# The w_out product's first row tile done in pieces between the last band heads

## The chip, the cores and the metric

The kernel runs on one core of a Trainium2 chip. The metric is the device time of one execution in microseconds (us). Five engines work side by side, each through its own queue in order, and wait for each other by semaphores: TensorE (PE), VectorE (DVE), ScalarE (ACT), GpSimd (POOL) and SyncE (SP, which here issues DMAs).

## The reference, cut to what matters

One layer of a hybrid encoder works on 1024 prompt rows and on 8 running streams (samples) of 16 rows each, 1152 rows in all, 1024 wide:

```
h   = rms_norm(x, g0)
... = split(h @ w_in)
o_fox  = fox_attention(q, k, v, log forget)   # 4 heads, causal, with the samples' cache of 256
o_lru  = rglru_block(...)
o_band = band_attention(q, k, v, rel_bias)    # 4 heads; a chunk of 64 sees itself and 8 before it
mix = concat([o_fox, o_lru, o_band]) @ w_out  # 1024 x 1024
x   = x + rms_norm(mix, g1)
h2  = rms_norm(x, g2)
gate, val = split(h2 @ w_up)
x   = x + rms_norm((gelu(dwconv(gate)) * val) @ w_down, g3)
```

All is float32. A big product is done in three passes of reduced type: each operand is split into a high part (a copy, by ACT) and a low part (value minus high part, by DVE), and PE sums high x high, high x low and low x high.

## The kernel before

The rows are cut into nine tiles of 128: 0 to 7 are the prompt, 8 the samples. After the w_in products comes the attention, a list of 44 units (`attention_steps`, `STEPS`, two steps each), written out by hand in `FOX_ORDER`, `BAND_ORDER` and two lists of places. A unit of kind pf or pb is two heads of one row tile q of the prompt (fox or band); pf needs q+1 blocks of 128 keys, pb at most five (q=0 one, q=1 two, q=2 three, q=3 four). Units sf and sb are two times two sample streams; kf, kb and kt turn keys.

The band's part was, as units 24 to 43: q=4, 4, 3, 3, key turn, 5, key turn, 5, sb (unit 32), 2, 2, 6, 6, sb (unit 37), 1, 1, 7, 7, 0, 0. Unit numbers m are those of the loop `for m in range(NUNIT)`, which each engine has.

All engines run through the units with a software pipeline. In iteration m

- PE turns the probabilities of unit m's first step (`turn_probs`), makes the scores of unit m+2 (`scores`), turns those of m's second step, and multiplies the turned ones of the unit before m with the values (`values`).
- DVE normalises the first step of m+1, takes both score tiles of m+2 out of PSUM with bias and row minimum (`take_scores`, L1226), normalises the second step of m+1 (L1237, L1246) and copies the output of the unit before m to `mix` (`take_output`, L1260).
- ACT copies the turned probabilities of m from PSUM (`turned_back`, L865) and exponentiates those of m+1 and m+2 (L873), or copies turned keys (L880).

`scores(m+2)` needs PSUM banks that DVE (or ACT, for keys) has taken unit m+1 from.

w_out is loaded by SP in eight halves q of 128 x 1024 elements (512 KB) into two buffers `raw`; load q waits for the low split of q-2. A split of a half is ACT's `split_hi` (L751) and DVE's `split_lo` (L1018). Halves 0 to 5 were split behind units 37 to 42 (`OUT_SPLITS`, from the last sb unit on, because w_hi and w_lo take the place of the samples' keys), 6 and 7 behind the loop. There also `mix_hi` (L909) and `mix_lo` (L1018) split the row tiles of `mix` into `act_hi` and `act_lo`; three tiles are split ahead. These buffers take the place of the keys, the values and the bias, so the first of them waited for the last output.

Then PE multiplies tile by tile, in the order 0 to 8, 48 matmuls each (L1731), and turns the finished row tile before it (`turn_y2`, L1426). For a tile ACT squares and takes the root (L945, L947), DVE multiplies with gains (L1326), adds the old rows `x_res` (L1329), ACT squares again (L952), DVE makes y2 (L1335); PE's turned y2 is split again (L930, L1018) and is the operand of the w_up product (L1436), which starts with the first six tiles. SP issues, behind the last w_out half: gains twice (when the last values are done), two halves of w_up (when w_out's halves 6 and 7 are split), x_res of tile 0, and then one x_res per tile.

```
            values(NOUT - 1)
...
            pe.wait_ge(att_out_used, NOUT)
            pe.wait_ge(w_lo_ready, R_OUT + 4)
            for t in range(NT):
                pe.wait_ge(lo_ready, NT + t + 1)
```

Of the kernel before, what the change touches and what calls it, by code (L numbers as in the profile page):

```python
# [119 lines left out]
def attention_steps():  # L120
# [21 lines left out]
    among_band = list(zip(pairs_of("kt") + pairs_of("sb"), (4, 5, 6, 10)))  # L142
# [5 lines left out]
BAND_ORDER = (4, 3, 5, 2, 6, 1, 7, 0)  # L148
# [14 lines left out]
OUT_SPLITS = [LAST["sb"] // 2 + q for q in range(6)]  # L163
# [66 lines left out]
def encoder_step(nc, i, o):  # L230
    with ExitStack() as ctx:
# [85 lines left out]
        with ExitStack() as s:  # L317
            wx_hi = sb("wx_hi", [P, 2048], F32R, s)
            wx_lo = sb("wx_lo", [P, 2048], F32R, s)
            x_res = sb("x_res", [P, D], F32, s)  # L320
            x1 = sb("x1", [P, D], F32, s)
            y2 = sb("y2", [P, D], F32, s)
# [150 lines left out]
        def mixed_banks(t):  # L473

            return 6 if t % 2 == 0 else 2

        def ring(r, tiles, spare):


            assert COUNT[FIRST["pb"]] % 4 == 0  # L480
# [30 lines left out]
        def _(sp):  # L511
# [26 lines left out]
            for q in range(8):  # L538
                r = R_OUT + q
                h, k0 = q // 4, 2 * (q % 4)  # L540
                if q == 0:
# [3 lines left out]
                          w_out[k0 * P:(k0 + 2) * P, h * 512:(h + 1) * 512].rearrange("(k p) c -> p k c", p=P))  # L545
# [43 lines left out]
        def _(pool):  # L589
# [131 lines left out]
            for t in range(NT):  # L721
                pool.wait_ge(x1_ready, t + 1)
                pool.dma_start(x1_dram[t * P:(t + 1) * P, :], x1[:, :]).then_inc(x1_stored, 16)
# [16 lines left out]
        def _(act):  # L740
# [150 lines left out]
            for m in range(NUNIT):  # L891
# [36 lines left out]
            def h2_half(t):  # L928
                act.wait_ge(y2_turned, t + 1)
                act.activation(act_hi[:, :, t * P:(t + 1) * P],  # L930
# [83 lines left out]
        def _(dve):  # L1014
# [247 lines left out]

            take_scores(0)
            take_scores(2)
            for m in range(NUNIT):
# [25 lines left out]
            def mix_lo(t):
                cols = slice(t * P, (t + 1) * P)
                dve.wait_ge(hi_ready, NT + t + 1)
                subtract(act_lo[:, :, cols], mix[:, :, cols], act_hi[:, :, cols]).then_inc(lo_ready, 1)
# [15 lines left out]
            def h2_lo_half(t):  # L1310
                cols = slice(t * P, (t + 1) * P)
# [4 lines left out]
            for t in range(NT):  # L1316
# [8 lines left out]
                step(dve.reciprocal(inv, inv))  # L1325
                step(dve.scalar_tensor_tensor(x1[:, :], PS[:, s0:s0 + 2, :].rearrange("p b c -> p (b c)"), inv,  # L1326
# [363 lines left out]

# [157 lines left out]
```

## Time and profile before

| | |
|---|---|
| median of three runs | 1504.38 us (1501.41 to 1505.44) |
| the profiled execution's own time | 1503.04 us |
| its span, first to last instruction | 1501.3 us |
| mean granted TensorE clock | 0.989 of full speed |
| PE busy | 1443.9 us (96%) |
| DVE busy | 715.2 us (48%) |
| ACT busy | 465.1 us (31%) |
| fox and band attention | about 302 to 470 us of the span |
| w_out product | about 472 to 588 us of the span |

The span is what the profile's times count in, from 0. Busy is time in which an engine worked at an instruction; PE's matmuls are pipelined, so the starts of two groups tell the cost of the first better than its length. A granted clock of 1.0 is 2.4 GHz, 0.5 is 1.2 GHz; a window that holds both shows a mean. In a timeline row the engine's line is followed by the operation, what it writes and reads, the count, and in brackets how long the engine had been idle and what released it.

### The profile page before, as it was taken

Reading aid. Unit: us, or ns where it says so; the run is one execution under the profiler, and the core shown is the slowest. Engines: PE = TensorE matmul, PEld = TensorE weight load, DVE = VectorE, ACT = ScalarE, POOL = GpSimd, SP = SyncE. Lnnn points to the kernel's source line nnn. Section 1 sums busy time; section 2 is a strip of 40 time slices with the busy share of each in tenths; the row PEclk is TensorE's granted clock in tenths of the full one; section 3 lists DMA queues with packets and bytes.
Section 4 is the critical chain, followed back from the end, with each engine's and each line's share of the span. In section 5 each row is a group of like instructions: output and inputs, shape, how many; then the busy total and the mean of one; then the engine's idle time right before and its main releaser. Section 6 shows DMA issues by size and latency. Waiting matters only on the chain.

```text
span 1501.3 us, 20856 instructions
## 1 busy us (share of the span) xinstructions
PE 1443.9 (96%) x8598; PEld 1310.3 (87%) x8598; DVE 715.2 (48%) x1196; ACT 465.1 (31%) x679; POOL 90.9 (6%) x129
## 2 busy tenths in 40 slices
PE   6999999989998999999999999999999999999994
PEld 6999988956776889999999999999999999999983
DVE  6433640167676555544444444353535353535346
ACT  6353341166566434312121212121212121212123
POOL 3000002122000011000000000000000000000006
PEclk9999999999999999999999999999999999999997
DMA  6210222225304233211111111011101010102033
GB/s 212 85 29 29 82 88 95 74 81 183 126 11 155 86 104 114 57 48 44 41 48 36 53 30 55 29 56 28 56 28 56 28 56 28 56 28 70 0 126 132
DMA packets 80006, 102.89 MB, mean 69 GB/s; under 512 B 3592, under 2 KB 63237, under 8 KB 79806
## 3 DMA queue, kind: packets, MB, share of 16 engines
q1 hardware_dynamic: 71744, 73.43, 15.7%
q0 software_dynamic: 8208, 28.69, 5.5%
q8 instruction: 40, 0.66, 0.2%
q14 instruction: 14, 0.11, 0.0%
HBM read 85.52 MB, written 16.58 MB: 68 GB/s over the span
## 4 chain that ended last, share of the span: by engine, by line
PE 93%; DVE 3%; ACT 2%; DMA 1%; issue 0%; POOL 0%; SPq 0%; ACTq 0%; DVEq 0%
PE PS L1436 50%; PE PS L1764 19%; PE PS L1505 7%; PE PS L1731 7%; PE PS L1426 4%; PE PS L1572 2%; PE PS L1665 2%; PE PS L1511 1%; DVE f_acc L1409 1%; PE PS L1595 1%; DVE act_lo L1018 0%; PE PS L1680 0%; DVE f_acc L1382 0%; DMA gains<-in_norm_g 0%; ACT w_hi L751 0%
## 5 line engine op out<-in xcount | busy, mean ns | idle before, releaser
L1436 PE MATMUL PS<-act_hi,w_hi 128*128 128x384 f32 x1152 | 208.4, 334 | 0.0
L1436 PE MATMUL PS<-act_lo,w_hi 128*128 128x384 f32 x1152 | 207.9, 334 | 0.0
L1436 PE MATMUL PS<-act_hi,w_lo 128*128 128x384 f32 x1152 | 207.9, 334 | 0.0
L1436 PEld LDWEIGHTS PS<-act_hi,w_hi 128*128 128x128 f32 x1152 | 200.8, 188 | 0.9
L1436 PEld LDWEIGHTS PS<-act_lo,w_hi 128*128 128x128 f32 x1152 | 200.4, 188 | 0.0
L1436 PEld LDWEIGHTS PS<-act_hi,w_lo 128*128 128x128 f32 x1152 | 200.4, 188 | 0.0
L1382 DVE TENSOR_TENSOR f_acc<-f_acc,PS 128x512 f32<-128x512 f32 x216 | 145.7, 687 | 79.7 <-PE PS L1764 79.6
L1764 PE MATMUL PS<-w_hi,f_hi 128*128 128x512 f32 x432 | 169.3, 392 | 4.8 <-ACT ffn_rows L999 4.8
L1764 PE MATMUL PS<-w_hi,f_lo 128*128 128x512 f32 x432 | 168.8, 391 | 0.0
L1764 PE MATMUL PS<-w_lo,f_hi 128*128 128x512 f32 x432 | 168.8, 391 | 0.0
L921 ACT ACTIVATE w_hi<-raw 128x1024 fp32r<-128x1024 f32 x72 | 72.3, 1051 | 224.9 <-PE PS L1764 219.4
L1764 PEld LDWEIGHTS PS<-w_hi,f_hi 128*128 128x128 f32 x432 | 81.4, 188 | 22.3 <-ACT ffn_rows L999 5.8
L1355 DVE COPY ffn_state<-gate_pad 128x2 f32 (+1 forms) x24 | 4.1, 169 | 202.7 <-ACT gate_pad L970 202.7
L1018 DVE TENSOR_TENSOR w_lo<-raw,w_hi 128x1024 fp32r<-128x1024 f32 x78 | 92.3, 1221 | 12.4 <-ACT w_hi L921 9.8
L1764 PEld LDWEIGHTS PS<-w_hi,f_lo 128*128 128x128 f32 x432 | 81.4, 188 | 17.0
L1764 PEld LDWEIGHTS PS<-w_lo,f_hi 128*128 128x128 f32 x432 | 81.4, 188 | 16.4
L1365 DVE TENSOR_TENSOR gate_pad<-PS,gate_conv 128x768 f32<-128x768 f32 x24 | 23.0, 958 | 152.4 <-PE PS L1436 151.1
L967 ACT ACTIVATE gate_pad<-PS 128x768 f32<-128x768 f32 x24 | 19.6, 817 | 195.5 <-PE PS L1436 195.5
L978 ACT ACTIVATE f_hi<-gate_pad 128x1152 fp32r<-128x1152 f32 x24 | 28.1, 1170 | 161.2 <-DVE gate_pad L1374 161.2
L732 POOL TENSOR_TENSOR f_acc<-f_acc,x_back 128x1024 f32<-128x1024 f32 x9 | 22.3, 2484 | 887.4 <-DMA x_back<-x_scratch 879.9
L974 ACT ACTIVATE gate_conv<-gate_conv 128x1168 f32<-128x1168 f32 x24 | 28.4, 1183 | 97.8 <-DVE gate_conv L1361 97.8
L1436 PE MATMUL PS<-act_hi,w_hi_all 128*128 128x384 f32 x288 | 54.1, 340 | 3.0 <-DVE act_lo L1018 2.7
(326 smaller groups left out, 1953.0 us busy)
## 6 DMA issues: line engine op xcount, KB each, us to landing
raw<-in_w_up SPq DMA_DIRECT2D x48, 512.0 KB, 4.6
raw<-in_w_down SPq DMA_DIRECT2D x24, 512.0 KB, 3.9
raw<-in_w_in SPq DMA_DIRECT2D x18, 512.0 KB, 4.7
x_scratch<-x POOLq DMA_DIRECT2D x9, 512.0 KB, 5.3
x_back<-x_scratch SPq DMA_DIRECT2D x1, 4608.0 KB, 14.3
x_in<-in_x_prompt SPq DMA_DIRECT2D x8, 512.0 KB, 5.3
raw<-in_w_out SPq DMA_DIRECT2D x8, 512.0 KB, 3.7
x_res<-in_x_prompt SPq DMA_DIRECT2D x8, 512.0 KB, 4.4
```

The source lines that it names most:

```text
L921: act.activation(w_hi[:, k // 2, (k % 2) * 1024:(k % 2 + 1) * 1024], raw[:, k % 2, :], ACT.Copy)\
L974: act.activation(gate_conv[:, :], gate_conv[:, :], ACT.Gelu_apprx_tanh).then_inc(gelu_ready, 1)
L978: act.activation(f_hi[:, c, :], gate_pad[:, FH:FH + T], ACT.Copy).then_inc(f_hi_ready, 1)
L1018: return dve.tensor_tensor(out, a, hi.bitcast(F32), ALU.subtract)
L1382: dve.tensor_tensor(acc, acc, PS[:, bank_of(q), :], ALU.add).then_inc(added, 1)
L1426: return pe.transpose(out, in_, ident[0:rows, 0:rows])
L1436: last = pe.matmul(PS[0:width, banks + c, 0:CW], w(wp, k), acts[ap][:, k, c * CW:(c + 1) * CW], start=(n == 0 and k == 0), stop=(n == 2 an ...
L1505: last = pe.matmul(bank_cols(b0 + c, width), acts[ap][:, k, t * P:(t + 1) * P], moving, start=(m == 0 and k == 0), stop=(m == 2 and k == K ...
L1572: last = pe.matmul(PS[:, 2 * s + b, 0:n_b * P], mix[rows, tile, q * P:(q + 1) * P], kt[rows, t, c0:c0 + n_b * P], start=not masked, stop=True,
L1665: last = pe.matmul(PS[64 * s:64 * s + 64, bank, 0:P], vals[:, k0 + b, HD * h:HD * (h + 1)], probs_t_of(2 * v + s)[:, b * P:(b + 1) * P], s ...
L1731: last = pe.matmul(PS[:, mixed_banks(t) + h, :], acts[ap][:, k, t * P:(t + 1) * P], wout_tile(wp, h, k), start=(m == 0 and k == 0), stop=( ...
L1764: last = pe.matmul(PS[:, bank_of(q), :], (f_hi, f_lo)[fp][:, k, t * P:(t + 1) * P], w, start=(k == 0 and m == 0), stop=(k == FG - 1 and m ...
```

## The change

The band's units 24 to 43 become: q=3, 3, 2, 2, key turn, 1, key turn, 1, sb (unit 32), 4, sb (unit 34), 4, 7, 7, 5, 5, 6, 6, 0, 0. w_out's halves are loaded and used in the other order of columns (the upper 512 first), 0 to 2 are split behind units 33 to 35 and 3 to 7 behind 39 to 43. The row tiles of the product are taken in the order 8, 4, 0, 1, 2, 3, 5, 6, 7. The first, of the samples, has buffers of its own, `early_hi` (written by ACT behind unit 38) and `early_lo` (DVE, behind 39), and goes to PSUM banks 0 and 1. Its 48 matmuls are twelve pieces of four: two in iteration 40 behind the scores of unit 42 and one behind its values, one behind 41's, one each in 42 and 43 between the two turns, one ahead of the last values and five behind them. Piece 0 waits for `early_lo`; pieces 0, 3, 6 and 9 for a further pair of halves. The last four steps keep their probabilities in the free part of `gains`, so that halves 6 and 7 can be split over the old place.

```diff
     among_fox = list(zip(pairs_of("kb") + pairs_of("kt") + pairs_of("sf"), (9, 11, 12, 14, 15, 16)))
-    among_band = list(zip(pairs_of("kt") + pairs_of("sb"), (4, 5, 6, 10)))
+    among_band = list(zip(pairs_of("kt") + pairs_of("sb"), (4, 5, 6, 7)))
...
 FOX_ORDER = (5, 7, 6, 4, 3, 2, 1, 0)
-BAND_ORDER = (4, 3, 5, 2, 6, 1, 7, 0)
+BAND_ORDER = (3, 2, 1, 4, 7, 5, 6, 0)
...
-OUT_SPLITS = [LAST["sb"] // 2 + q for q in range(6)]
+LAST_SB = LAST["sb"] // 2
+OUT_SPLITS = [LAST_SB - 1, LAST_SB, LAST_SB + 1] + list(range(NUNIT - 5, NUNIT))
+EARLY_HI_AT, EARLY_LO_AT = LAST_SB + 4, LAST_SB + 5
+W_OUT_ORDER = (8, 4, 0, 1, 2, 3, 5, 6, 7)
+EARLY_AFTER_SCORES = {NUNIT - 4: 2, NUNIT - 2: 1, NUNIT - 1: 1}
+EARLY_AFTER_VALUES = {NUNIT - 4: 1, NUNIT - 3: 1, NUNIT - 1: 2}
...
+            sb("probs_gap", [P, 2 * 2048], F32, s)
+            early_hi = sb("early_hi", [P, KD, P], F32R, s)
+            early_lo = sb("early_lo", [P, KD, P], F32R, s)
...
+            y2 = sb("y2", [P, D], F32, s)
+            x1 = sb("x1", [P, D], F32, s)
             x_res = sb("x_res", [P, D], F32, s)
...
+            if t == 0:
+                return 0
             return 6 if t % 2 == 0 else 2
...
+        def mix_parts(i):
+
+            t = W_OUT_ORDER[i]
+            cols = slice(t * P, (t + 1) * P)
+            if i == 0:
+                return mix[:, :, cols], early_hi[:, :, :], early_lo[:, :, :]
+            return mix[:, :, cols], act_hi[:, :, cols], act_lo[:, :, cols]
...
+            if r >= NREAL - 4:
+                return gains[:, spare, BANDW + P * s:BANDW + P * (s + 1)]
...
+        def out_half(buffers, q):
+
+            c0 = (q % 2) * 1024
+            return buffers[0][:, q // 2, c0:c0 + 1024] if q < 6 else buffers[1][:, c0:c0 + 1024]
...
-                          w_out[k0 * P:(k0 + 2) * P, h * 512:(h + 1) * 512].rearrange("(k p) c -> p k c", p=P))
+                          w_out[k0 * P:(k0 + 2) * P, (1 - h) * 512:(2 - h) * 512].rearrange("(k p) c -> p k c", p=P))
...
-                    sp.wait_ge(att_out_used, NOUT)
+                    sp.wait_ge(att_out_used, outputs_until(LAST["sb"]))
...
-                sp.dma_start(x_res[:, :], rows_of(xp, xs, t)).then_inc(res_loaded, 16)
+                sp.dma_start(x_res[:, :], rows_of(xp, xs, W_OUT_ORDER[t])).then_inc(res_loaded, 16)
...
+            def mix_hi(i):
+                source, hi, _ = mix_parts(i)
+                act.activation(hi, source, ACT.Copy).then_inc(hi_ready, 1)
...
+                if q == 6:
+                    act.wait_ge(probs_turned, NREAL - 4)
+                split_hi(R_OUT + q, out_half((w_hi, wx_hi), q))
...
+                if m == EARLY_HI_AT:
+                    act.wait_ge(att_out_used, outputs_until(LAST["sb"]))
+                    mix_hi(0)
...
+            act.wait_ge(scores_ready, NSTEP)
+            act.wait_ge(att_out, NOUT - 2)
+            mix_hi(1)
...
-            mix_hi(0)
-            for q in (6, 7):
-                split_hi(R_OUT + q, wx_hi[:, (q - 6) * 1024:(q - 5) * 1024])
-            for t in range(1, MIX_AHEAD):
+            for t in range(2, MIX_AHEAD):
                 mix_hi(t)
...
+            def mix_lo(i):
+                source, hi, lo = mix_parts(i)
+                dve.wait_ge(hi_ready, NT + i + 1)
+                subtract(lo, source, hi).then_inc(lo_ready, 1)
...
+                    if q == 6:
+                        dve.wait_ge(att_out, NOUT - 2)
+                    split_lo(R_OUT + q, out_half((w_hi, wx_hi), q), out_half((w_lo, wx_lo), q))
+                if m == EARLY_LO_AT:
+                    mix_lo(0)
+            mix_lo(1)
             take_output(NOUT - 1)
-
...
-            mix_lo(0)
-            for q in (6, 7):
-                half = slice((q - 6) * 1024, (q - 5) * 1024)
-                split_lo(R_OUT + q, wx_hi[:, half], wx_lo[:, half])
-            for t in range(1, MIX_AHEAD):
+            for t in range(2, MIX_AHEAD):
                 mix_lo(t)
-            dve.wait_ge(gain2_loaded, 32)
...
+                if t == 0:
+                    dve.wait_ge(gain2_loaded, 32)
...
+            def wout_tile(part, h, k):
+                half = out_half(((w_hi, wx_hi), (w_lo, wx_lo))[part], 4 * (1 - h) + k // 2)
+                return half[:, (k % 2) * 512:(k % 2 + 1) * 512]
+
+            def early_product(n):
+
+                for piece in range(early_done[0], early_done[0] + n):
+                    h, k0, m = 1 - piece // 6, 4 * (piece // 3 % 2), piece % 3
+                    if piece == 0:
+                        pe.wait_ge(lo_ready, NT + 1)
+                    if piece == 6:
+                        pe.wait_ge(scores_used[0], NUNIT)
+                    if m == 0:
+                        pe.wait_ge(w_lo_ready, R_OUT + 2 * (piece // 3) + 2)
+                    ap, wp = ((0, 0), (0, 1), (1, 0))[m]
+                    for k in range(k0, k0 + 4):
+                        last = pe.matmul(PS[:, mixed_banks(0) + h, :], (early_hi, early_lo)[ap][:, k, :],
+                                         wout_tile(wp, h, k), start=(m == 0 and k == 0),
+                                         stop=(m == 2 and k == KD - 1))
+                    if piece == 11:
+                        last.then_inc(mixed, 1)
+                early_done[0] += n
+
...
                     scores(m + 2)
+                early_product(EARLY_AFTER_SCORES.get(m, 0))
                 if is_real(m):
                     turn_probs(COUNT[2 * m + 1])
                     if COUNT[2 * m] >= 2:
                         values(COUNT[2 * m] // 2 - 1)
+                if m < NUNIT - 1:
+                    early_product(EARLY_AFTER_VALUES.get(m, 0))
+            early_product(1)
             values(NOUT - 1)
+            early_product(12 - early_done[0])
...
-            pe.wait_ge(w_lo_ready, R_OUT + 4)
-            for t in range(NT):
+            for t in range(1, NT):
...
-                for h in range(2):
-                    if t == 0 and h == 1:
-                        pe.wait_ge(w_lo_ready, R_OUT + 8)
+                for h in (1, 0):
                     for m, (ap, wp) in enumerate(((0, 0), (0, 1), (1, 0))):
                         for k in range(KD):
-                            last = pe.matmul(PS[:, mixed_banks(t) + h, :], acts[ap][:, k, t * P:(t + 1) * P],
+                            last = pe.matmul(PS[:, mixed_banks(t) + h, :], acts[ap][:, k, c0:c0 + P],
...
-            pe.wait_ge(h2_lo, 2 * NT // 3)
+            pe.wait_ge(h2_lo, 2 * NT // 3 + 1)
```

## Rows read from the trace of the kernel before

**Rows 1.** The page, part 4: the chain that ended last, by engine.
```profile
PE 93%; DVE 3%; ACT 2%; DMA 1%; issue 0%; POOL 0%; SPq 0%; ACTq 0%; DVEq 0%
```

**Rows 2.** Windows; columns: start:end length, busy (count) of PE to POOL, clock, DMA.
```profile
398.36:455.30 56.94, 55.88 (x700) 41.28 (x700) 43.91 (x145) 38.95 (x88) 1.76 (x2) 1.00 0.19 66
455.30:469.80 14.50, 10.38 (x90) 7.36 (x88) 11.87 (x35) 10.75 (x24) 0.00 (x0) 0.88 0.39 143
469.80:485.00 15.20, 12.41 (x48) 10.18 (x49) 7.29 (x7) 5.91 (x6) 0.00 (x0) 0.89 0.70 211
```

**Rows 3.** The same view, finer stretches.
```profile
360.00:380.00 20.00, 17.39 (x150) 12.24 (x148) 12.63 (x44) 9.67 (x28) 1.83 (x2) 0.92 0.31 99
456.00:458.60 2.60, 0.57 (x5) 0.33 (x4) 2.24 (x7) 2.56 (x5) 0.00 (x0) 0.99 0.49 184
458.60:462.00 3.40, 3.36 (x18) 2.58 (x18) 2.61 (x10) 2.73 (x6) 0.00 (x0) 0.50 0.43 151
472.60:476.00 3.40, 3.40 (x9) 2.71 (x10) 2.78 (x3) 2.89 (x4) 0.00 (x0) 0.56 0.99 286
```

**Rows 4.** The chain in order of time: start, us, what.
```profile
463.30 3.96 DMA raw<-in_w_out
...
471.22 1.24 DVE act_lo L1018
...
496.07 0.87 PE PS L1426 x8
496.94 10.90 PE PS L1731 x48
```

**Rows 5.** Timeline of PE; in brackets the idle time before, and its releaser.
```profile
417.60 1.35 PE L1572 MATMUL PS<-kt_b,mix 64*128 64x512 f32 x8 [0.66 <-ACT kt_s L880]
...
450.20 0.65 PE L1680 MATMUL PS<-probs_t,cache_v 128*64 128x16 f32 x16
...
453.02 1.35 PE L1572 MATMUL PS<-kt_b,mix 64*128 64x512 f32 x8
...
456.89 0.49 PE L1572 MATMUL PS<-kt_b,mix 64*128 64x128 f32 x4 [0.81 <-DVE stat L1226]
458.64 1.30 PE L1426 MATMUL PS<-ident,probs 128*128 128x128 f32 x5 [1.25 <-ACT probs_t L865]
...
463.06 0.74 PE L1426 MATMUL PS<-ident,gains 128*128 128x128 f32 x5 [0.46 <-ACT probs_t L865]
463.73 1.31 PE L1665 MATMUL PS<-probs_t,v_b 128*64 128x128 f32 x20
...
472.59 3.49 PE L1731 MATMUL PS<-w_hi,act_hi 128*128 128x512 f32 x8 [2.83 <-DVE act_lo L1018]
...
485.02 1.98 PE L1731 MATMUL PS<-w_hi,act_hi 128*128 128x512 f32 x8
```

**Rows 6.** Timeline of DVE, one wide unit and a split.
```profile
455.18 0.82 DVE L1226 CUSTOM_DVE_ANT_0 probs<-PS,band_bias 128x640 f32<-128x640 f32 x1
...
456.67 0.08 DVE L1226 DVE_READ_ACCUMULATOR2_ANT stat<- 128x1 f32 x1
...
457.33 0.28 DVE L1260 COPY mix<-PS 128x128 f32<-128x128 f32 x1
457.94 1.23 DVE L1018 TENSOR_TENSOR w_lo<-raw,w_hi 128x1024 fp32r<-128x1024 f32 x1 [0.33 <-ACT w_hi L751]
459.08 0.16 DVE L1237 RECIPROCAL stat<-stat 128x1 f32<-128x1 f32 x1
```

**Rows 7.** Timeline of ACT in the same unit: exponent, then split.
```profile
456.04 0.83 ACT L873 ACTIVATE probs<-probs,stat 128x640 f32<-128x640 f32 x1 [0.88 <-DVE stat L1226]
...
456.87 1.04 ACT L751 ACTIVATE w_hi<-raw 128x1024 fp32r<-128x1024 f32 x1
```

**Rows 8.** DMA issues, 380 to 480; last column: median us to landing.
```profile
gains<-in_norm_g SPq DMA_DIRECT2D x2, 512.0 KB, 6.0
...
x_res<-in_x_prompt SPq DMA_DIRECT2D x1, 512.0 KB, 7.4
```

More of the change, by code:

```diff
@@ L317, in encoder_step @@
         with ExitStack() as s:
+            sb("probs_gap", [P, 2 * 2048], F32, s)
+            early_hi = sb("early_hi", [P, KD, P], F32R, s)
+            early_lo = sb("early_lo", [P, KD, P], F32R, s)
+        with ExitStack() as s:
             wx_hi = sb("wx_hi", [P, 2048], F32R, s)
             wx_lo = sb("wx_lo", [P, 2048], F32R, s)
+            y2 = sb("y2", [P, D], F32, s)
+            x1 = sb("x1", [P, D], F32, s)
             x_res = sb("x_res", [P, D], F32, s)
-            x1 = sb("x1", [P, D], F32, s)
-            y2 = sb("y2", [P, D], F32, s)
         cum_rows = probs[0:H, 0, 0:SEQ]
@@ L473, in mixed_banks @@
         def mixed_banks(t):
+            if t == 0:
+                return 0
             return 6 if t % 2 == 0 else 2
+        def mix_parts(i):
[4 more added lines that the diff above has]
+            return mix[:, :, cols], act_hi[:, :, cols], act_lo[:, :, cols]
         def ring(r, tiles, spare):
-            assert COUNT[FIRST["pb"]] % 4 == 0
+            assert COUNT[FIRST["pb"]] % 4 == 0 and NREAL % 4 == 0
+            assert all(STEPS[n][0] == "pb" and STEPS[n][2] == 0 for n in REAL[NREAL - 4:])
             s = r % 4
@@ L722, in _ @@
                 pool.wait_ge(x1_ready, t + 1)
-                pool.dma_start(x1_dram[t * P:(t + 1) * P, :], x1[:, :]).then_inc(x1_stored, 16)
+                pool.dma_start(tile_rows(x1_dram, W_OUT_ORDER[t], 1), x1[:, :].rearrange("p (c d) -> p c d", c=1)).then_inc(x1_stored, 16)
                 if t == ZERO_AT:
@@ L929, in h2_half @@
                 act.wait_ge(y2_turned, t + 1)
-                act.activation(act_hi[:, :, t * P:(t + 1) * P],
+                c0 = W_OUT_ORDER[t] * P
+                act.activation(act_hi[:, :, c0:c0 + P],
                                PS[:, 4:6, :].rearrange("p b (k c) -> p (b k) c", c=P), ACT.Copy).then_inc(h2_hi, 1)
@@ L1285, in _ @@
                     q = OUT_SPLITS.index(m)
-                    cols = slice((q % 2) * 1024, (q % 2 + 1) * 1024)
-                    split_lo(R_OUT + q, w_hi[:, q // 2, cols], w_lo[:, q // 2, cols])
-            take_output(NOUT - 1)
[L1291 to L1294, printed above, removed]
-            mix_lo(0)
-            for q in (6, 7):
-                half = slice((q - 6) * 1024, (q - 5) * 1024)
-                split_lo(R_OUT + q, wx_hi[:, half], wx_lo[:, half])
-            for t in range(1, MIX_AHEAD):
+                    if q == 6:
[4 more added lines that the diff above has]
+            mix_lo(1)
+            take_output(NOUT - 1)
+            for t in range(2, MIX_AHEAD):
                 mix_lo(t)
-            dve.wait_ge(gain2_loaded, 32)
             def split_group_half(r, k):
@@ L1310, in h2_lo_half @@
             def h2_lo_half(t):
-                cols = slice(t * P, (t + 1) * P)
+                t0 = W_OUT_ORDER[t]
+                cols = slice(t0 * P, (t0 + 1) * P)
                 dve.wait_ge(h2_hi, t + 1)
@@ L1689, in values @@
                 last.then_inc(att_out, 1)
+            def wout_tile(part, h, k):
[18 more added lines that the diff above has]
+                early_done[0] += n
+            early_done = [0]
             pe.wait_ge(out_used, NO)
@@ L1713, in turn_y2 @@
                 last.then_inc(y2_turned, 1)
-            def wout_tile(part, h, k):
-                q = 2 * h + k // 4
-                w = (w_hi, w_lo)[part][:, q, :] if q < 3 else (wx_hi, wx_lo)[part][:, :]
-                return w[:, (k % 4) * 512:(k % 4 + 1) * 512]
             pe.wait_ge(att_out_used, NOUT)
-            pe.wait_ge(w_lo_ready, R_OUT + 4)
-            for t in range(NT):
+            for t in range(1, NT):
+                c0 = W_OUT_ORDER[t] * P
                 pe.wait_ge(lo_ready, NT + t + 1)
@@ L1725, in _ @@
                     pe.wait_ge(x1_ready, t - 1)
-                for h in range(2):
-                    if t == 0 and h == 1:
-                        pe.wait_ge(w_lo_ready, R_OUT + 8)
+                for h in (1, 0):
                     for m, (ap, wp) in enumerate(((0, 0), (0, 1), (1, 0))):
                         for k in range(KD):
-                            last = pe.matmul(PS[:, mixed_banks(t) + h, :], acts[ap][:, k, t * P:(t + 1) * P],
+                            last = pe.matmul(PS[:, mixed_banks(t) + h, :], acts[ap][:, k, c0:c0 + P],
                                              wout_tile(wp, h, k), start=(m == 0 and k == 0),
                                              stop=(m == 2 and k == KD - 1))
-                    if t == NT - 1 and h == 0:
+                    if t == NT - 1 and h == 1:
                         last.then_inc(low_half_mixed, 1)
                 last.then_inc(mixed, 1)
-                if t >= 1:
-                    turn_y2(t - 1)
+                turn_y2(t - 1)
             def up_product(c, half, chunks):
```

4 lines of the change are left out of this document (removed).

## The prediction

> **What bounds the kernel now.** I read the chain that ended last first: 93% of it is TensorE (PE) work [rows 1], so what counts is where PE stands idle or runs at its lower clock. The change touches only the last 20 of 44 attention units and the first row tile of the w_out product, so I cut that part into windows next [rows 2]. The reader is to see there the elapsed time, PE's busy time and the granted clock of each. From 398.36 (the band's first unit, m=24) to 455.3 PE is busy 55.88 of 56.94 us: PE sets the pace and only 1.06 us is lost. From 455.3 to 469.8 it is busy 10.38 of 14.50, at a mean clock of 0.88. From 469.8 to 485.0, where the first row tile's product ends, it is busy 12.41 of 15.20, at 0.89. Outside these windows nothing the change touches waits.
>
> The fine windows [rows 3] show where the 0.88 and 0.89 come from. After a stretch that was nearly empty (0.57 busy of 2.60) PE worked 3.36 us at clock 0.50, the lower of its two levels, 1.2 GHz. After the gap ahead of the product, 3.40 us at 0.56. That work would have taken 1.7 and 1.5 us less at 2.4 GHz. A third stretch, 360 to 380, was idle for 2.61 us and shows 0.92.
>
> The chain in that part [rows 4] and the timelines say who made PE wait. Ahead of the product everything is in series: last copy of mix, ACT's act_hi, DVE's act_lo, then PE at 472.59, 2.83 us idle [rows 5]. In the last units PE waits 0.81 us for a score tile that DVE takes late and 1.25 us for ACT's probs_t, which stands behind a w_hi split [rows 5, 7]. There the units are narrow (two blocks of keys or one) and leave PE little work beside the splits.
>
> So what is there to be won: idle 1.06 + 4.12 + 2.79 = 7.97 us and clock 1.7 + 1.5 = 3.2 us, 11.2 us in all. PE's work at full clock in 398.36 to 485.0 is 78.67 - 3.2 = 75.5 us. The change moves work and adds none to PE (12 pieces of 4 matmuls are the same 48 matmuls), so this sum stays.
>
> **Part 1: the new order of the band.** The narrow units (q=3, 2, 1) come first, the samples' second pair moves from unit 37 to 34, and eight wide units (q=4, 7, 5, 6) follow; the last pair stays q=0. From the timelines a unit of five blocks costs PE two turns of 0.67 (463.06 to 463.73), scores of 1.3 (453.02) and values of 1.3 (463.73) [rows 5], 3.9 us. DVE needs for it two takes (455.18 to 456.67, 1.49), two normalisations of 0.66 (456.67 to 457.33) and a copy of 0.28 [rows 6], 3.1 us. So wide units are PE-bound with 0.8 us to spare; a split (1.14 on DVE, 457.94 to 459.08 [rows 6]) takes it 0.3 us over. Scaled by blocks, a unit of two costs PE some 2 us and DVE 1.8 (an estimate from the same rows), so the narrow ones are near balance. In the new order these stand beside key turns and sample units, which have PE work of their own. The weak point is scores right behind a key turn, which wait for ACT's copy: 417.60 shows 0.66 us [rows 5]; with a narrow unit between two key turns I take 0.8. Bounds: 0, and what 360 to 380 shows, where narrow units stand among key turns too (2.61 us idle and 1.6 of clock [rows 3]). I take 1.2 us of waits for m=24 to 38 against 1.06 before. That is at 398.36 + the same work.
>
> **Part 2: the splits.** Six splits behind units 37 to 42 and two behind the loop become three behind 33 to 35 and five behind 39 to 43. Each is one ACT copy of 1.04 and one DVE subtraction of 1.14 [rows 6, 7]. The first three lie beside units of which two also carry the values of sample pairs (four groups like that of 450.20 with four short ones each [rows 5], 2.5 us of PE work), so they are hidden: DVE's queue for 33, 34 and 35 is about 5.2, 4.2 and 4.2 us, PE's 5.1, 3.5 and 5.1, and the excess of one is taken up by the next. SP's loads follow them: load q waits for split q-2 and landed 3.96 us behind it [rows 4]. q2 to q6 have an iteration or more of about 4 us; q7, behind q5's split at m=41, has one narrow unit and the pieces. By hand q7's low part ends about where piece 9 wants it: 0 to 1 us late, I take 0.2. Their cost if the cover is gone is their own 1.14 each.
>
> **Part 3: mix_hi and mix_lo of the samples' tile.** ACT's 1.0 at m=38 is hidden: its two exponents of 0.83 [rows 7] and two shorter copies leave room in 3.9 us. DVE's subtraction at m=39 is not. Count from the start of unit 39's first turn: scores(41) start at 0.7, DVE takes from 2.1 to 3.6, normalises to 4.25 and copies to 4.45. ACT comes to w_hi of q=3 only behind probs_t and the exponent, 4.3 to 5.3, so DVE's split runs to 6.5 and mix_lo(0) to 7.65; PE may start at 7.8 (0.13 lies between act_lo's end, 471.22 + 1.24, and PE's start [rows 4, 5]). PE comes to piece 0 behind 3.9 us of unit 39, a turn and a narrow scores: at 5.0. So it stands 2.7 us. Behind the waiting matmul in PE's queue are the turn of 40b and values(39), and for those DVE's copy and its next split wait. Bounds: 0 if DVE runs ahead by as much, 4 if ACT's split is one step later. I take 2.7.
>
> A gap of 2.8 us at 469.8 was followed by low clock, and one of 2.0 idle in 2.6 too [rows 2, 3]. So I add 1.5 us for the pieces behind this wait. Bounds 0 and 1.7. The Trainium skill ("TensorE: Matmul & The Clock Gate", section on what is happening in Part 1) has it that the gate looks at fixed stretches which don't start with the kernel; a gap may then fall so that it costs nothing. By that rule the sum is 1.5 us better in some layouts; the trace had low clock behind each gap of this size, so I keep 1.5.
>
> **Part 4: the pieces and the end.** Twelve pieces at 0.91 (10.90 for 48 matmuls [rows 4]) fill PE where it waited: one or two behind units 40 to 43, one ahead of the last values, five behind. The waits of 0.81 and 1.25 and the rest of the 4.12 us idle there go, as does the serial 2.83 with its clock: while PE does the last five pieces, DVE does mix_lo(1) and ACT mix_hi(2). Pieces between short steps break PE's stream; 0.2 us for it, bound 0.17 each (1.2).
>
> **Part 5: what comes behind.** SP issues gains, two halves of w_up and x_res as before, but now only 5 pieces (4.6 us) lie between the last values and the end of tile 0. gains took 6.0 and x_res 7.4 us [rows 8]. With the w_up half waiting for q7's split, x_res lands about 9.5 us behind the last values, and DVE wants it at about 9: 0.3 late. PE needs y2 only behind tile 1's 10.9 us product, some 2 us later than that gives. So this costs nothing; were the landing 3 us later, PE would stand 1 us. From tile 1 on the rhythm (10.90 + 0.87 [rows 4]) is unchanged; the order of the tiles asks the up product for seven tiles instead of six, and these are there before the last product ends. The separate banks 0 and 1, the new places of the last probs and of x1, y2 cost nothing: their users are through.
>
> **The sum.** End of tile 0: 398.36 + 75.5 + 1.2 + 2.7 + 1.5 + 0.4 = 479.7, against 485.0: 5.3 us less. The profiled execution took 1503.04 us (span 1501.3); 1503.04 - 5.3 = 1497.7. The median shown is 1.3 us above that execution, which would give 1499.1; I take the middle, 1498.4.
>
> **The rivals.** (A) The forecast, 3.5 to 7 us won: 0.50. (B) DVE runs ahead or the clock holds: 6.8 to 9.7 us won, time about 1496; for it speaks that only one wait is left that is over 1 us, against it DVE's sum at unit 39 and the rows after each gap: 0.24. (C) The gain is mostly given back: the change does what it says, but the narrow units beside the key turns lose 1 to 2 us more (as at 360 to 380 [rows 3]), or q7 and x_res are late by 1 to 2 us each; about 2.5 us won, 1501: 0.17. (D) The early product doesn't take the place of any wait, because each piece only pushes the heads' chain that the next waits for; then the 7.97 us of idle stay and only the 2.8 and its clock go or stay; near 1503: 0.03. (E) The other side: the clock. The wait at piece 0 starts a low stretch, and the short waits between heads and pieces keep PE at 1.2 GHz. Each us of work at that level costs one more; without clock my gain is 6.8 us, so from 6.8 us of work at low clock on the kernel is slower. Some 19 us of PE work lie between piece 0 and the end of tile 0; with 10 of them low the time is 1503.04 + 3.2 = 1506.2. For it: three low stretches in this part already. Against: PE was back at full clock after 3.4 us each time though its units left it idle (463.06 on) [rows 2, 5]. 0.06. The same page of the Trainium skill (section "A second HAM failure mode: psum-queue depth-cycling") describes just this, small idle times between groups of matmuls that make the clock swing; the trace's last units do not show it.
>
> **How the numbers follow.** 0.3% (4.5 us) is about what a measurement of this kernel can tell from no change. B and 0.7 of A pass it: faster 0.24 + 0.35 = 0.59; the rest of A, C and D make 0.35 within; E 0.06. The range goes from B's best (9.7 won: 1494.0) to D (1503.5), which leaves out E and the tails of the executions' scatter of about 2 us.
>
> **What would show it.** Right: the first w_out matmuls (128x512) behind scores(42) start after a wait of 2 to 3.5 us released by DVE's subtraction into early_lo, with about 3.4 us at 0.5 behind it; tile 1's product follows tile 0's with no gap; tile 0 ends some 5 us sooner and everything behind keeps its durations. Wrong: waits over 1 us in units 27 to 38, a wait at piece 9 or at the first turn of y2, or no low clock.

## The result and the profile after

The changed kernel takes 1496.86 us (median of nine runs, 1494.91 to 1499.44) against 1504.4 of the kernel before beside it. The ratio is 0.9957, 95% interval 0.9944 to 0.9969: 6.5 us faster, between 4.7 and 8.4. The ratio compares all the executions and not the two medians, which lie 7.5 us apart; one of the nine of the kernel before, at 8167.8 us, is left out of it. The profiled execution took 1496.86 us, 6.18 less than that of before.

The page of the changed kernel, span and chain by engine (as [rows 1]):

```profile
span 1495.1 us, 20861 instructions
PE 94%; DVE 3%; ACT 2%; issue 0%; DMA 0%; POOL 0%; SPq 0%; ACTq 0%; DVEq 0%
```

The span is 6.2 us shorter. Where it went is told by the windows of the part that was changed (the columns as in [rows 2]). Unit 24 starts at 398.29 here (398.36 before); tile 0's product ends at 479.03 (485.02 before).

```profile
398.29:451.55 53.26, 51.76 (x658) 38.62 (x659) 43.79 (x142) 37.55 (x84) 1.75 (x2) 1.00 0.27 91
451.55:456.70 5.15, 5.13 (x49) 3.64 (x47) 3.79 (x11) 5.04 (x10) 0.00 (x0) 1.00 0.00 0
456.70:459.30 2.60, 0.02 (x3) 0.01 (x1) 2.42 (x3) 1.54 (x4) 0.00 (x0) 1.00 0.06 10
459.30:465.00 5.70, 5.70 (x44) 4.57 (x46) 2.93 (x10) 2.12 (x5) 0.00 (x0) 1.00 0.25 90
465.00:479.03 14.03, 13.57 (x98) 10.22 (x96) 8.86 (x22) 9.41 (x18) 0.00 (x0) 1.00 0.47 144
```

PE's busy time is 51.76 + 5.13 + 0.02 + 5.70 + 13.57 = 76.2 us in 80.7, all of it at clock 1.00. Before it was 78.67 in 86.66, at mean clocks of 0.88 and 0.89 in the last two windows [rows 2]. So idle time fell from 7.97 to 4.6 us and the low clock, 3.2 us, is gone; PE's work at full clock rose from 75.5 to 76.2. Some 0.4 us of this is only moved into the stretch: the scores of its first two units are made ahead of it, and those units had five blocks of keys before and have four now. The rest, 0.3, is what the pieces between the heads cost (the run with the old order of row tiles below tells the two apart). Together 3.4 + 3.2 - 0.7 = 5.9 us. Behind tile 0 nothing moved; the chain of the changed kernel has the same steps as in [rows 4] and reaches the first up product at 573.45, where it was at 579.43 before, 5.98 us sooner (the row of before, then the row of after):

```profile
579.43 8.35 PE PS L1436 x48
```

```profile
573.45 8.35 PE PS L1467 x48
```

The timeline of PE through the tail (as [rows 5]) shows the new wait and the joints:

```profile
451.55 0.76 PE L1457 MATMUL PS<-ident,probs 128*128 128x128 f32 x5
...
456.22 0.49 PE L1603 MATMUL PS<-kt_b,mix 64*128 64x128 f32 x4
459.29 1.20 PE L1738 MATMUL PS<-w_hi,early_hi 128*128 128x512 f32 x4 [2.58 <-DVE early_lo L1049]
460.32 1.09 PE L1738 MATMUL PS<-w_lo,early_hi 128*128 128x512 f32 x4
461.25 0.71 PE L1457 MATMUL PS<-ident,probs 128*128 128x128 f32 x5
...
465.76 0.74 PE L1457 MATMUL PS<-ident,gains 128*128 128x128 f32 x5 [0.46 <-DVE gains L1277]
...
478.12 1.07 PE L1738 MATMUL PS<-wx_hi,early_lo 128*128 128x512 f32 x4
479.03 1.98 PE L1784 MATMUL PS<-w_hi,act_hi 128*128 128x512 f32 x8
...
489.91 1.03 PE L1457 MATMUL PS<-ident,y 128*128 128x128 f32 x8
```

Unit 39 starts at 451.55. The first piece waits 2.58 us for `early_lo`. The step from it to the next piece is 1.03 us and from there 0.93: a piece that follows another sort of work takes about 0.12 more than the 0.91 of one in a row (478.12 to 479.03). The turn behind a piece is over sooner, though: 0.63 us lie between the starts of the turn at 464.17 and of the scores behind it, 0.70 at 455.52 and 456.22. The next wait is 0.46. Tile 1 follows tile 0, and y2's turn follows tile 1, with no gap.

Who made the first piece wait is in DVE's timeline (as [rows 6]) and, below it, in ACT's (as [rows 7]):

```profile
453.63 0.82 DVE L1257 CUSTOM_DVE_ANT_0 probs<-PS,band_bias 128x640 f32<-128x640 f32 x1 [0.75 <-PE PS L1603]
...
455.91 0.29 DVE L1291 COPY mix<-PS 128x128 f32<-128x128 f32 x1
456.88 1.23 DVE L1049 TENSOR_TENSOR w_lo<-raw,w_hi 128x1024 fp32r<-128x1024 f32 x1 [0.68 <-ACT w_hi L778]
458.02 1.22 DVE L1049 TENSOR_TENSOR early_lo<-mix,early_hi 128x1024 fp32r<-128x1024 f32 x1
459.15 0.15 DVE L1268 RECIPROCAL stat<-stat 128x1 f32<-128x1 f32 x1
```

```profile
454.38 0.70 ACT L892 ACTIVATE gains<-PS 128x640 f32<-128x640 f32 x1
454.98 0.82 ACT L900 ACTIVATE probs<-probs,stat 128x640 f32<-128x640 f32 x1
...
455.80 1.04 ACT L778 ACTIVATE w_hi<-raw 128x1024 fp32r<-128x1024 f32 x1
```

The reader is to see DVE's queue run without a break from the take of unit 41's scores (453.63) to the end of `early_lo`, but for 0.68 us in which it waits for `w_hi` of half 3. ACT made that behind the copy of the turned probabilities of unit 39's second step (454.38) and an exponent (454.98). PE was ready for the piece at 456.7.

### The profile page after: what moved, and what is told of

Same layout as the page of the kernel before. It is cut to its first block, busy times and chain, and to the rows that moved or that the text cites. A ratio compares the mean times of both kernels' runs of the same rounds, so it can differ in the third digit from the quotient of the medians.

```text
span 1495.1 us, 20861 instructions
## 1 busy us (share of the span) xinstructions
PE 1441.7 (96%) x8598; PEld 1307.8 (87%) x8598; DVE 715.9 (48%) x1196; ACT 464.4 (31%) x679; POOL 90.7 (6%) x129
## 4 chain that ended last, share of the span: by engine, by line
PE 94%; DVE 3%; ACT 2%; issue 0%; DMA 0%; POOL 0%; SPq 0%; ACTq 0%; DVEq 0%
PE PS L1467 50%; PE PS L1816 19%; PE PS L1536 7%; PE PS L1784 6%; PE PS L1457 4%; PE PS L1603 2%; PE PS L1696 2%; PE PS L1738 1%; PE PS L1542 1%; DVE f_acc L1440 1%; PE PS L1711 1%; PE PS L1626 0%; DVE f_acc L1413 0%; DMA gains<-in_norm_g 0%; DVE act_lo L1049 0%
```

## The experiments

All stretches below run from the start of unit 24 to the end of tile 0's product, read from the timelines as above. They leave out how an execution came to unit 24 (396.2 to 400.4 us into the span), which varies from one execution to the next. A stretch is that of one execution; the ratio is from five to twelve executions of each kernel and eight to eighteen of the kernel before, run beside it.

| kernel | unit 24 | tile 0 ends | stretch | ratio to before (95%) |
|---|---|---|---|---|
| before | 398.36 | 485.02 | 86.66 | |
| before, once more | 396.76 | 486.38 | 89.62 | |
| changed | 398.29 | 479.03 | 80.74 | 0.9957 (0.9944 to 0.9969) |
| changed, once more | 397.86 | 479.92 | 82.06 | 0.9964 (0.9952 to 0.9976) |
| parts split late | 396.19 | 482.66 | 86.47 | 0.9992 (0.9981 to 1.0003) |
| all pieces behind | 398.00 | 479.55 | 81.55 | 0.9966 (0.9954 to 0.9978) |
| old order of tiles | 396.81 | 479.54 | 82.73 | 0.9974 (0.9961 to 0.9986) |
| mix_lo(0) ahead of the split | 400.42 | 479.24 | 78.82 | 0.9945 (0.9933 to 0.9958) |
| pieces 0 to 2 later | 397.26 | 476.21 | 78.95 | 0.9944 (0.9924 to 0.9964) |
| mix_lo(0) behind unit 38 | 397.22 | 475.31 | 78.09 | 0.9937 (0.9923 to 0.9950) |
| the same, splits moved too | 396.36 | 476.07 | 79.71 | 0.9940 (0.9922 to 0.9958) |
| the same, every gap filled | 396.33 | 473.97 | 77.64 | 0.9935 (0.9918 to 0.9951) |

**The changed kernel once more.** No edit.

> The changed kernel itself, to see which terms repeat. Theory (the early product fills PE's waits in the tail; what is left is the wait for early_lo): PE stands 2.5 to 2.7 us ahead of the first w_out matmuls behind scores(42) again, tile 0 ends about 479 us into the span, time about 6 us below the kernel before. On the clock two theories differ: that a wait of this size never costs clock here (rival) expects 1.00 behind it in every profile; that the low stretch comes or not by when the wait falls expects 0.5 for some 3.4 us behind it in some of the profiles with such a wait.

The wait is 2.58 us again, but behind it PE runs at the lower level, and the stretch is 1.32 us longer. First its PE timeline, then its windows:

```profile
458.86 2.07 PE L1738 MATMUL PS<-w_hi,early_hi 128*128 128x512 f32 x4 [2.58 <-DVE early_lo L1049]
```

```profile
458.80:462.30 3.50, 3.44 (x10) 2.72 (x11) 0.84 (x5) 0.00 (x0) 0.00 (x0) 0.57 0.43 150
462.30:466.00 3.70, 3.70 (x39) 2.98 (x37) 2.24 (x6) 2.22 (x5) 0.00 (x0) 1.00 0.00 0
```

The same wait in the same kernel had no low stretch behind it in the first profile. So the low stretch comes with one execution and not with another; the rival that a wait of this size is free is out. In time this second set of executions is 5.4 us faster than the kernel before (0.9964, interval 3.6 to 7.2 us), against 6.5 in the first; the two can't be told apart.

**mix_lo(0) ahead of the low split.**

```diff
+                if m == EARLY_LO_AT:
+                    mix_lo(0)
                 if m in OUT_SPLITS:
...
-                if m == EARLY_LO_AT:
-                    mix_lo(0)
```

> In iteration 39 DVE's mix_lo(0) comes ahead of the low split of half 3. Theory (PE stands for DVE's queue): mix_lo(0) then starts when the copy to mix is done (456.2 instead of 458.0) and PE's wait falls from 2.6 to about 0.7 us, the split of half 3 is late for nobody; tile 0 ends about 1.8 us sooner, 4 to 5 us less at most if a low stretch of clock goes with it. Rival (the wait is slack that comes back in the narrow units, where DVE's chain sets the pace): under 0.5 us.

```profile
459.51 1.19 PE L1738 MATMUL PS<-w_hi,early_hi 128*128 128x512 f32 x4 [0.67 <-DVE early_lo L1049]
```

The wait fell by 1.91 us to 0.67 and the stretch by 1.92. Nothing came back later: DVE's queue at unit 39 was the price, us for us. The clock was 1.00 throughout the stretch.

**mix_lo(0) one unit sooner.**

```diff
-EARLY_HI_AT, EARLY_LO_AT = LAST_SB + 4, LAST_SB + 5
+EARLY_HI_AT, EARLY_LO_AT = LAST_SB + 3, LAST_SB + 4
```

> mix_hi(0) behind unit 37 and mix_lo(0) behind unit 38, where DVE has 0.75 us idle in a wide unit. Theory: DVE's queue in iteration 38 is then 3.1 + 1.1 us against PE's 3.9, so it starts iteration 39 about 0.3 us late, PE's wait at the first piece goes (0 to 0.3 us), tile 0 ends 2.3 to 2.6 us sooner than in the changed kernel. Rival (slack that comes back): under 0.5 us.

```profile
455.15 0.49 PE L1603 MATMUL PS<-kt_b,mix 64*128 64x128 f32 x4
455.57 1.20 PE L1738 MATMUL PS<-w_hi,early_hi 128*128 128x512 f32 x4
```

In PE's timeline the first piece (455.57) follows the scores of unit 42 (455.15) with no wait, and the stretch is 2.65 us shorter than in the changed kernel. The time says so too: the ratio is 0.9937 (0.9923 to 0.9950) against 0.9964 (0.9952 to 0.9976) of the changed kernel timed beside it, and the intervals don't meet.

**All pieces behind the last values.**

```diff
-EARLY_AFTER_SCORES = {NUNIT - 4: 2, NUNIT - 2: 1, NUNIT - 1: 1}
-EARLY_AFTER_VALUES = {NUNIT - 4: 1, NUNIT - 3: 1, NUNIT - 1: 2}
+EARLY_AFTER_SCORES = {}
+EARLY_AFTER_VALUES = {}
...
-            early_product(1)
             values(NOUT - 1)
```

> All twelve pieces behind the last values; order, splits and buffers as in the changed kernel. Theory 1 (the pieces fill waits that would be there): the waits of the narrow units come back, 0.5 to 1.3 us each at three or four places, about 4 us with their clock, against the 2.6 us wait and 0.6 us of joints that go; tile 0 ends 1 to 2 us later. Rival (the samples' tile needs no last output, so it is enough that its parts are ready): the waits are about 1.5 to 2 us in all, tile 0 ends 1 to 2 us sooner than in the changed kernel, and the interleaving by itself brings nothing.

```profile
457.29 0.74 PE L1457 MATMUL PS<-ident,probs 128*128 128x128 f32 x5 [0.87 <-ACT probs_t L892]
...
459.66 0.77 PE L1457 MATMUL PS<-ident,probs 128*128 128x128 f32 x5 [0.39 <-DVE probs L1277]
...
462.02 0.74 PE L1457 MATMUL PS<-ident,gains 128*128 128x128 f32 x5 [1.17 <-ACT probs_t L892]
...
465.13 0.30 PE L1457 MATMUL PS<-ident,gains 128*128 128x128 f32 x1 [0.88 <-ACT gains L892]
...
467.48 0.30 PE L1457 MATMUL PS<-ident,gains 128*128 128x128 f32 x1 [0.54 <-ACT gains L892]
```

These are all of PE's waits from unit 40 on: 0.87 + 0.39 + 1.17 + 0.88 + 0.54 = 3.85 us. In the changed kernel they are 2.58 + 0.46 = 3.04. The stretch is 0.81 us longer than the changed kernel's, a little less than Theory 1 gave, and the clock was 1.00 throughout. It is also 0.51 us shorter than that of the changed kernel's second profile, with its low stretch, and in time the two kernels can't be told apart (0.9966 and 0.9964). So as they are placed, the pieces take away all but 0.46 of 3.85 us of waits, bring 2.58 of their own, and gain little. With the pieces where they are and `early_lo` ready (the run before) the stretch is 3.46 us shorter than with all behind, and the ratio 0.9937 against 0.9966.

**The samples' tile split late as well.** As the last edit, and

```diff
-EARLY_HI_AT, EARLY_LO_AT = LAST_SB + 4, LAST_SB + 5
+EARLY_HI_AT, EARLY_LO_AT = NUNIT - 1, NUNIT - 1
```

> As the run with all pieces behind the last values, and the samples' tile is split only in iteration 43, behind the low split of half 7 (ACT's part ahead of its copy of half 7). What is left of the change is the order, the early splits of halves and the two halves taken out of the end. Theory (what the samples' tile gives is that its parts need no last output, so the chain mix, act_hi, act_lo, PE is not in series): PE waits 3.5 to 4.5 us at the first piece (half 7 loaded, 1.0, 1.1, 1.1), most likely with a low stretch behind; from unit 24 to the end of tile 0 it takes 84 to 87 us, against 81.5 with all behind, 80.7 in the changed kernel, 86.7 before. Rival (order and split places make the gain): under 82.5.

```profile
470.17 2.08 PE L1738 MATMUL PS<-w_hi,early_hi 128*128 128x512 f32 x4 [4.52 <-DVE early_lo L1049]
```

```profile
470.10:473.50 3.40, 3.33 (x8) 2.66 (x9) 2.28 (x4) 2.00 (x2) 0.00 (x0) 0.52 1.10 311
```

PE waits 4.52 us and then starts at low clock (the window). The stretch is 86.47, that of the first profile of the kernel before, and the time is not to be told from it. So without the early parts the change brings nothing. That the first tile's parts are ready when the heads end brings 4.9 us (86.47 to 81.55): 3.5 of waits and 1.4 of PE's busy time, by the clock. The ratios agree (0.9992 and 0.9966, intervals that don't meet). The interleaving as it is brings 0.8 more by the first profile of the changed kernel, and nothing that the times show.

The run doesn't show that the new order and the new places of the splits are worth nothing by themselves. The wait ahead of the product is 4.52 us here and 2.83 in the kernel before, because `early_lo` is written behind the low split of half 7, whose load landed late. The waits between the heads from unit 40 on are shorter in return (2.8 us, 4.1 before). With the tile split in iteration 43 but ahead of half 7 the rest of the change could come out better; that was not run.

**The old order of row tiles.**

```diff
-BAND_ORDER = (3, 2, 1, 4, 7, 5, 6, 0)
+BAND_ORDER = (4, 3, 5, 2, 6, 1, 7, 0)
```

> The band's row tiles in the order of the kernel before (4, 3, 5, 2, 6, 1, 7, 0), with the samples' units at 32 and 34 and everything else as in the changed kernel; ahead of the pieces stand two narrow units instead of two wide ones. Theory (PE's iteration 39 is 1.2 us shorter, DVE's queue stays): the wait for early_lo grows from 2.6 to about 3.1 to 3.8 us, and 38 and 39 bring short waits; tile 0 ends 0.5 to 2 us later. Rival (the order of the wide tiles is what makes the gain): over 4 us later.

```profile
443.53 0.74 PE L1457 MATMUL PS<-ident,probs 128*128 128x128 f32 x5 [0.48 <-ACT probs_t L892]
...
446.78 0.74 PE L1457 MATMUL PS<-ident,gains 128*128 128x128 f32 x5 [0.25 <-DVE probs L1277]
...
458.89 1.20 PE L1738 MATMUL PS<-w_hi,early_hi 128*128 128x512 f32 x4 [2.97 <-DVE early_lo L1049]
```

```profile
458.80:460.00 1.20, 1.11 (x5) 0.94 (x6) 0.87 (x5) 0.00 (x0) 0.00 (x0) 1.00 0.76 256
460.00:463.50 3.50, 3.50 (x18) 2.58 (x16) 0.61 (x4) 0.75 (x2) 0.00 (x0) 0.52 0.16 60
```

The wait at the first piece is 2.97, a little under the 3.1 to 3.8 expected, and units 36 to 39 bring waits of 0.48 and 0.25 (the first two rows). Behind 460 a low stretch follows. The stretch from unit 24 is 82.73, 1.99 longer than in the first profile of the changed kernel, of which the windows' 3.50 us at 0.52 are about 1.7. PE is busy 77.44 us in it, which is 75.8 at full clock, against 76.2 in the changed kernel: the wider scores of the first two units, 0.4 us, lie ahead of the stretch. The kernel before had the same work in its stretch at 75.5, without the pieces in between; so these cost 0.3. The idle time is 5.29 us against 4.56. The new order is worth about 0.7 us by the profiles, too little to see in time (0.9974 and 0.9964, intervals that overlap); the rival's 4 us are out.

**Pieces 0 to 2 behind the values of iteration 40.**

```diff
-EARLY_AFTER_SCORES = {NUNIT - 4: 2, NUNIT - 2: 1, NUNIT - 1: 1}
-EARLY_AFTER_VALUES = {NUNIT - 4: 1, NUNIT - 3: 1, NUNIT - 1: 2}
+EARLY_AFTER_SCORES = {NUNIT - 2: 1, NUNIT - 1: 1}
+EARLY_AFTER_VALUES = {NUNIT - 4: 3, NUNIT - 3: 1}
```

> Pieces 0 to 2 all behind the values in iteration 40, so PE turns 40b and multiplies unit 39's values before it needs early_lo. Theory: of the 2.6 us wait none is left, but the turn of 40b waits 0.9 us for ACT's probs_t as in the run with all pieces behind; tile 0 ends 1.5 to 1.9 us sooner than in the changed kernel. Rival (the wait is DVE's chain and only moves): under 0.5 us.

```profile
456.55 0.74 PE L1457 MATMUL PS<-ident,probs 128*128 128x128 f32 x5 [0.87 <-ACT probs_t L892]
...
462.93 0.74 PE L1457 MATMUL PS<-ident,gains 128*128 128x128 f32 x5 [0.46 <-ACT probs_t L892]
```

(The edit also drops an entry for the last unit that the loop never used.) These are PE's two waits in the tail: the 0.87 us that the pieces had covered, and 0.46 at the turn of 41b as in the changed kernel. The stretch is 1.79 us shorter than the changed kernel's. It is a second way to the same end as mix_lo(0) sooner, and 0.86 us worse in its stretch, by the first of these waits.

**Splits moved out of the tail, every gap with a piece.** As mix_lo(0) behind unit 38, and

```diff
-OUT_SPLITS = [LAST_SB - 1, LAST_SB, LAST_SB + 1] + list(range(NUNIT - 5, NUNIT))
+OUT_SPLITS = [LAST_SB - 1, LAST_SB, LAST_SB + 1, LAST_SB + 2, LAST_SB + 3, NUNIT - 4, NUNIT - 2, NUNIT - 1]
...
+EARLY_AFTER_SCORES = {NUNIT - 4: 1, NUNIT - 3: 1, NUNIT - 2: 1, NUNIT - 1: 1}
+EARLY_AFTER_VALUES = {NUNIT - 4: 1, NUNIT - 3: 1}
```

> mix_hi(0) and mix_lo(0) behind 37 and 38, halves 3 and 4 split behind 36 and 37 and 5 behind 40, one piece in every gap of 40 and 41 (behind the scores and behind the values). Theory: against the run with only the sooner mix_lo(0) the 0.46 us wait at the turn of 41b goes too, joints stay; 0.3 to 0.5 us better in the profile, not to be told apart in time (ratio to the kernel before about 0.993). Rival (DVE, with split and mix_lo(0) in 36 to 38, now paces the wide units): 1 to 2 us worse.

```profile
449.39 0.74 PE L1457 MATMUL PS<-ident,probs 128*128 128x128 f32 x5 [1.34 <-ACT probs_t L892]
```

My theory was wrong here, and the rival's size right though not its engine: the stretch is 1.62 us longer than with mix_lo(0) sooner alone. PE waits 1.34 us for ACT, whose queue got `mix_hi(0)` and the copy of half 4 in one iteration. In time the two can't be told apart (0.9940 and 0.9937).

**Every gap with a piece, splits where they were.** As mix_lo(0) behind unit 38, and of the last edit only the two lines on the pieces.

> The run with mix_lo(0) behind unit 38, and one piece in each gap of 40 and 41 (behind the scores and behind the values) instead of two, one, none, one; halves split where the changed kernel has them. Theory: the 0.46 us wait at the turn of 41b goes, one joint of 0.13 more; from unit 24 to the end of tile 0 77.8 us against 78.1, not to be told apart in time. Rival (DVE's norm of 41b is late whatever stands ahead, so the wait only moves): 78.1 or more.

```profile
460.72 0.71 PE L1457 MATMUL PS<-ident,gains 128*128 128x128 f32 x5
```

The 0.46 us wait at the turn of 41b is gone (the row has no bracket), and PE has no wait from unit 32 to the end of tile 0. The stretch is 77.64, the shortest of all, and the median 1492.63 us (1490.5 to 1495.92). From the sooner mix_lo(0) alone it can't be told apart in time. By its stretch it is the version to keep.

**The kernel before once more.** No edit.

> The kernel before, profiled once more. If the low clock behind a wait comes by the place of the wait, the same two stretches at 0.5 show (behind 456 to 458.6 and at the product's start). If it comes or goes from one execution to the next, one of them may be missing or longer; the waits themselves (0.81, 1.25, 2.83 us) are the same in both cases.

The waits are the same 0.81, 1.25 and 2.83 us, and the stretch is 2.96 us longer: PE is busy 3.9 us longer and idle 0.95 us less. The windows show why:

```profile
457.00:460.50 3.50, 3.48 (x18) 2.57 (x18) 2.67 (x11) 2.72 (x6) 0.00 (x0) 0.50 0.46 147
460.50:464.00 3.50, 3.34 (x22) 2.69 (x23) 2.38 (x9) 2.23 (x7) 0.00 (x0) 0.50 0.36 107
464.00:467.50 3.50, 3.04 (x24) 2.22 (x22) 2.14 (x6) 2.54 (x6) 0.00 (x0) 0.50 0.14 52
467.50:471.00 3.50, 3.04 (x24) 1.86 (x20) 1.63 (x3) 0.78 (x3) 0.00 (x0) 0.50 0.45 150
...
474.00:477.30 3.30, 3.29 (x8) 2.64 (x9) 3.30 (x4) 3.30 (x4) 0.00 (x0) 0.54 0.68 230
477.30:480.00 2.70, 2.70 (x13) 2.25 (x12) 1.56 (x2) 0.43 (x1) 0.00 (x0) 1.00 1.10 328
```

PE is at the lower level from about 457 to 477, some 20 us, where the first profile had two stretches of 3.4 us [rows 3]. The idle time shrinks at the three short waits behind the first two: they were 0.46, 0.88 and 0.66 us, and are 0.16, 0.46 and 0.46 now that PE comes to them later.

## Why the prediction was right, and which term was not

By its own steps; 5.3 us less was forecast for the stretch, 5.9 were measured, and the time (1496.86) lies in the range. That the two sums are so near is in part luck: the clock, taken as 1.5 us, cost nothing in the first profile, and 1.0 us went the other way (0.3 more of waits up to unit 38, 0.26 more in place of piece 9's wait, and 0.4 of PE work that the sum left out). In the second profile, where the clock cost 1.3, the stretch is 82.06, 4.6 us less than in the first profile of the kernel before.

- *The work that "stays":* the prediction took PE's work in the stretch as 75.5 us in both kernels. It is 76.2, of which 0.4 are scores of the first two units that the new order brings into the stretch; the prediction didn't look at how wide these units are.

- *Part 1, the order:* 1.2 us of waits for m=24 to 38 forecast, 1.50 measured (53.26 - 51.76). The one behind a key turn, taken as 0.8, is 0.99:

```profile
415.08 0.70 PE L1603 MATMUL PS<-kt_b,mix 64*128 64x256 f32 x4 [0.99 <-ACT kt_s L907]
```

- *Part 2, the splits:* in units 33 to 38 PE waits for none, and piece 9 did not wait. Instead of 0.2 us there, 0.46 stand at the turn of 41b, where DVE's split of half 4 is ahead of the normalisation.
- *Part 3, the wait for early_lo:* 2.7 forecast, 2.58 and 2.58 measured. The way to it was right as well: DVE's two takes, normalisation, copy, ACT's late w_hi, split, mix_lo.
- *Part 3, the clock behind it:* this is the term that was wrong in size, +1.5 us. In the first profile it cost nothing, in the second 1.32. "No low clock" was one of the prediction's own signs of being wrong, and the first profile has it. The prediction had both sizes as bounds and put the whole cost into the sum, because each gap of that size in its one profile had a low stretch behind it. (It counts three such stretches "in this part"; there are two, the third, 360 to 380, lies ahead of unit 24.) One profile could not show that this changes from execution to execution. The Trainium skill ("TensorE: Matmul & The Clock Gate", section "What's actually happening") has it that the gate's stretches are free-running. The two profiles of the changed kernel fit that: 1.00 and a mean of 0.57 behind the same wait.
- *Part 4, the joints:* 0.2 forecast. Seven lots follow other work and take 0.12 more each, 0.8 in all, but the turns behind some of them are shorter; by PE's busy time the pieces cost 0.3 (75.8 in the run with the old order, 75.5 before). The run with all pieces behind has hardly a joint and the same busy time as the changed kernel, 76.2. The term was about right.
- *Part 5, behind tile 0:* PE never waited, as forecast, but with less room. DVE's timeline has x_res 1.64 us late, where 0.3 were expected (the load took 8.5 us, 7.4 before [rows 8], and landed at about 485.0):

```profile
482.18 1.28 DVE L1357 SCALAR_TENSOR_TENSOR x<-PS,stat,gains 128x1024 f32<-128x1024 f32 x1
485.10 1.23 DVE L1360 TENSOR_TENSOR x<-x,x_res 128x1024 f32<-128x1024 f32 x1 [1.64 <-DMA x_res<-in_x_sample]
...
488.07 1.29 DVE L1366 SCALAR_TENSOR_TENSOR y<-x,stat,gains 128x1024 f32<-128x1024 f32 x1
```

y2 is done at about 489.3, and PE turns it at 489.91: some 0.6 us of room where the prediction had 2.
- *The rivals:* B had two halves, DVE ahead or the clock holding. DVE was not ahead; the clock held in one of two profiles, and the gain of that one (6.2 us) still lies in A's own range. C: the narrow units cost 0.3 more than forecast, not 1 to 2. D is out: the idle time fell from 7.97 to 4.6 us, and the run with all pieces behind shows 3.85 us of waits that the pieces take the place of. E needed 6.8 us of PE work at low clock in the changed kernel; its two profiles had none and 3.5 us at a mean of 0.57. The kernel before showed in its second profile something like what E is about, short waits with 20 us of low clock. The same page of the Trainium skill, section "A second HAM failure mode: psum-queue depth-cycling", says that small idle times between groups of matmuls make the clock swing. The prediction held against it that the trace didn't show it, and one trace was too few for that; but the second trace doesn't swing either, it stays at 0.50 from 457 to 471. Whether the small idle times caused this is not shown: the first profile has the same waits and came back to 1.00 after 3.4 us.

The timed gain (6.5 us, interval 4.7 to 8.4) is above the 5.3 forecast but holds it, and in the second set of executions it is 5.4. So there is no difference left that asks for a cause. Nor did the first profile of the kernel before show too little low clock, as far as three digits tell: its mean clock over the whole span is 0.989, and that is the average of the 49 executions of this kernel timed beside the experiments (0.986 to 0.991). The 18 timed executions of the changed kernel average 0.991, as its first profile has. The second profile of the kernel before, at 0.986, is at the low end.

## What to carry to other kernels

Work moved into another stage is paid for in the queue of the engine that prepares its operands: count that queue from the last common event, instruction by instruction, and place the preparation one round before the consumer (2.65 us here, for one line). Such a gain has two parts: having the first operands ready when the stage before ends (4.9 us here) and the interleaving (0.8 by one profile as it was placed, 3.5 to 3.9 once the operands were ready in time). Tell the two apart before tuning the second. Profile both kernels twice before a term for the clock goes into a sum.

## What the runs showed of the hardware

- The same wait of 2.58 us in the same kernel had 1.00 behind it in one profile and 3.5 us at a mean of 0.57 in another. Waits of 2.97 and 4.52 us had 0.52 behind them for 3.4 to 3.5 us, once with 1.1 us of full-clock work first.
- Shorter waits had no low clock behind them in the changed kernels: 0.67 alone, and five of 0.39 to 1.17 us between 456 and 468 in the run with all pieces behind. In both profiles of the kernel before, 0.81 and 1.25 us close together had 0.50 behind them, for 3.4 us in one and for 14 us and more in the other.
- About 20 us at 1.2 GHz in the second profile of the kernel before made the stretch only 3.0 us longer than two stretches of 3.4 us did. PE was busy 3.9 us longer and idle 0.95 less.
- A lot of four 128x512 matmuls takes 0.91 us behind another such lot and about 0.12 more behind turns, scores or values; a turn of five blocks takes 0.63 us behind such a lot and 0.67 to 0.70 elsewhere (start to start).
